# Every second step of the second layer's forgetting attention reordered to values, turning, scores; value products one step later

## What is computed

```
def fox_attention(q, k, v, Fq, Fk, q_off):          # second layer only
    def block(args):                                # one block of 128 queries
        qb, fqb, qpos = args
        s = jnp.einsum('bqhd,bkhd->bhqk', qb, k) * FOX_SCALE
        s = s + jnp.swapaxes(fqb, 1, 2)[..., None] - Fk_t
        s = jnp.where(kpos[None, :] <= qpos[:, None], s, -jnp.inf)
        p = jax.nn.softmax(s, axis=-1)
        return jnp.einsum('bhqk,bkhd->bqhd', p, v)

def mem_attend(q, k, v):                            # both layers
    p = jax.nn.softmax(jnp.einsum('blhd,bmhd->bhlm', q, k) * MEM_SCALE, axis=-1)
    return jnp.einsum('bhlm,bmhd->blhd', p, v)

x = x + jnp.concatenate([op, om], axis=-1) @ w_out[i]
x = x + swiglu(x, g_ffn[i], w_gu[i], w_down[i])
```

## Time and profile before

| | |
|---|---|
| median of 3 executions | 1226.25 us (1225.66 to 1226.43) |
| span of the profiled execution, first to last instruction | 1224.1 us |
| TensorE busy, of that span | 1208.8 us (99%) |
| VectorE, ScalarE busy | 983.7 us (80%), 649.6 us (53%) |
| second layer's attention (704.4 to 779.3 us) | 74.9 us |
| of it, one chunk of four forgetting pairs | 10.32 us |
| TensorE clock granted, mean | 0.998 of full speed |

### The profile page before, as it was taken

The page is one execution under the profiler, slowest core; times in us unless marked ns, Lnnn a source line. Parts: engine busy times, 40 slices in busy tenths (PEclk is TensorE's granted clock), DMA queues, the critical chain, the costliest instruction groups (busy, mean ns, idle before and its releaser), DMA issues.

```text
span 1224.1 us, 23230 instructions
## 1 busy us (share of the span) xinstructions
PE 1208.8 (99%) x9048; PEld 1167.6 (95%) x9048; DVE 983.7 (80%) x1605; ACT 649.6 (53%) x1175; POOL 88.9 (7%) x124
## 2 busy tenths in 40 slices
PE   8999999999999999999999999999999999999997
PEld 8998999999999999999989986899999999999997
DVE  6777558999999999976776377557999999999972
ACT  6657335454554555555754377534555555555542
POOL 2000000001001001102001100000001001100103
PEclk9999999999999999999999999999999999999999
DMA  7343222236325434525444310132134433532622
GB/s 229 121 138 106 67 74 86 74 88 141 96 87 121 109 96 106 132 86 158 138 129 124 99 40 2 36 87 86 53 101 116 114 95 96 125 104 83 163 62 86
DMA packets 198012, 124.08 MB, mean 101 GB/s; under 512 B 6419, under 2 KB 190131, under 8 KB 197648
## 3 DMA queue, kind: packets, MB, share of 16 engines
q1 hardware_dynamic: 185792, 101.23, 28.0%
q0 software_dynamic: 11920, 21.30, 7.7%
q10 hardware_dynamic: 192, 0.06, 0.0%
HBM read 106.67 MB, written 7.94 MB: 94 GB/s over the span
## 4 chain that ended last, share of the span: by engine, by line
PE 94%; DVE 2%; ACT 1%; DMA 1%; issue 1%; SPq 0%; DVEq 0%; ACTq 0%
PE ACCP L1854 32%; PE ACCP L1875 25%; PE MISC L1875 23%; PE ACCP L1967 3%; PE ACCP L2127 3%; PE ACCP L2098 2%; PE MISC L1891 1%; PE MISC L2069 1%; PE MISC L2082 1%; PE MISC L1897 1%; DMA XR<-in_x_prompt 1%; PE MISC L2086 1%; DVE XL L1579 0%; DVE ACC L1587 0%; DVE WL L1433 0%
## 5 line engine op out<-in xcount | busy, mean ns | idle before, releaser
L1102 ACT ACTIVATE WH<-RAW 128x1024 fp32r<-128x1024 f32 (+2 forms) x149 | 144.1, 967 | 140.9 <-PE ACCP L1854 120.6
L1120 ACT ACTIVATE EH<-SB 128x1024 fp32r<-128x1024 f32 (+1 forms) x116 | 112.6, 970 | 161.4 <-DVE SB L1458 80.6
L1433 DVE TENSOR_TENSOR WL<-RAW,WH 128x1024 fp32r<-128x1024 f32 (+2 forms) x148 | 166.2, 1123 | 17.5 <-ACT WH L1102 16.4
L1464 DVE TENSOR_TENSOR EL<-SB,EH 128x1024 fp32r<-128x1024 f32 (+1 forms) x116 | 128.7, 1109 | 5.5 <-ACT EH L1120 3.4
L1854 PE MATMUL ACCP<-XH,WH 128*128 128x288 f32 x512 | 111.2, 299 | 0.5 <-DVE XL L1579 0.5
L1854 PE MATMUL ACCP<-XH,WL 128*128 128x288 f32 x512 | 109.7, 296 | 0.0
L1854 PE MATMUL ACCP<-XL,WH 128*128 128x288 f32 x512 | 109.6, 296 | 0.0
L1875 PE MATMUL MISC<-BH,EH 128*128 128x288 f32 x360 | 106.7, 296 | 0.0
L1875 PE MATMUL ACCP<-BH,EH 128*128 128x288 f32 x360 | 106.6, 296 | 0.0
L1875 PE MATMUL ACCP<-BL,EH 128*128 128x288 f32 x360 | 106.2, 295 | 0.0
L1875 PE MATMUL MISC<-BL,EH 128*128 128x288 f32 x360 | 106.2, 295 | 0.0
(11 more groups left out here) (362 smaller groups left out, 3414.2 us busy)
## 6 DMA issues: line engine op xcount, KB each, us to landing
RAW<-in_w_gu SPq DMA_DIRECT2D x88, 512.0 KB, 4.1
RAW<-in_w_down SPq DMA_DIRECT2D x48, 384.0 KB, 3.9
RAW<-in_w_in SPq DMA_DIRECT2D x16, 512.0 KB, 5.1
RAW<-in_w_mem_kv SPq DMA_DIRECT2D x16, 512.0 KB, 3.7
RAW<-in_w_out SPq DMA_DIRECT2D x16, 512.0 KB, 3.9
X<-PC POOLq DMA_DIRECT2D x48, 144.0 KB, 2.9
RAW<-in_w_down SPq DMA_DIRECT2D x16, 256.0 KB, 2.7
RAW<-in_w_kv SPq DMA_DIRECT2D x8, 512.0 KB, 3.7
```

What stands on the lines that cost most here:

```text
L1102: a.activation(panel_in(WH, w % SPLIT_SLOTS, p), panel_in(RAW, p % RAW_SLOTS, p), ACT.Copy).then_inc(split_ready(w, True)[0], 1)
L1120: a.activation(EH[:, first:first + n, 0:nh], mixtures(s)[:, first:first + n, 0:nh], ACT.Copy).then_inc(block_hi, n)
L1433: v.tensor_tensor(panel_in(WL, w % SPLIT_SLOTS, p), panel_in(RAW, p % RAW_SLOTS, p), panel_in(WH, w % SPLIT_SLOTS, p), ALU.subtract).then_ ...
L1464: v.tensor_tensor(EL[:, first:first + n, 0:nh], mixtures(s)[:, first:first + n, 0:nh], EH[:, first:first + n, 0:nh], ALU.subtract).then_in ...
```

## The change

In the second layer, values and closing come one step later (values of pair n-4, closing of pair n-5), and the loop has one step more. And in each odd step whose scores are of forgetting attention (n = 11, 13, ... 29) the order is values of pair n-4, turning of pair n-2, scaling of pair n-1, and only then scores and exponentials of pair n. Even steps, memory steps and the steps behind the last scores keep scores, turning, values. The first layer is as it was.

```
-        for n in range(len(twos) + 4):
-            new, scaled, turned, valued, closed = (lag(n, by) for by in range(5))
+        late = layer == DEPTH - 1
+        for n in range(len(twos) + 4 + late):
+            new, scaled, turned = (lag(n, by) for by in range(3))
+            valued, closed = lag(n, 3 + late), lag(n, 4 + late)
+            flipped = new and new.att == "fox" and n % 2 == 1
             if closed and closed.last:
                 add("branch_hi", two=closed)
+            if flipped:
+                if valued:
+                    add("values", two=valued, g=before["g"])
+                for e in range(2):
+                    add("turn_probs", r=turned.rows[e], first=False, g=before["g"])
+                add("scale_probs", two=scaled)
             if new:
                 add("scores", two=new, m=before["jobs"], s=before["s"], g=before["g"], i=n)
                 for what in ((first, second)[n] if n < 2 else ()):
                     what()
             if closed and closed.last:
                 add("branch_lo", two=closed)
-            if scaled:
+            if scaled and not flipped:
                 add("scale_probs", two=scaled)
             for e in range(2):
                 if new:
                     add("exp", r=new.rows[e])
-                if turned:
+                if turned and not flipped:
                     add("turn_probs", r=turned.rows[e], first=turned.first and e == 0, g=before["g"])
-            if valued:
+            if valued and not flipped:
                 add("values", two=valued, g=before["g"])
```

## The result

| | before | the change |
|---|---|---|
| median of 4 executions | 1226.12 us (1225.66 to 1226.43) | 1235.34 us (1233.89 to 1235.75) |
| span of the profiled execution | 1224.1 us | 1234.0 us |
| second layer's attention, first scores to first matmul of the projection | 74.92 us | 84.74 us |
| one chunk, third to fourth (transposes of tile 3 to transposes of tile 3) | 10.32 us | 12.04 us |

The change is slower: ratio 1.0073, 95% interval 1.0061 to 1.0084, that is +9.2 us against a forecast of +7.1. The attention is 9.82 us longer and the span 9.9, so everything lies there. The projection behind it takes 56.19 us in both.

What follows compares the result with a forecast made beforehand. TensorE's own work bounds the kernel, so waits reach the end whole. 4.6 + 2.1 + 1.0 + 1.55 - 0.8 - 1.3 = +7.1 us on the 1224.1 us span: 1231.2, median 1233.3 us; range 1227.0 to 1236.5.

Steps and rivals of the forecast that it cites:

- ahead of tile 2: Transposes of tile 2 after tile 3 wait for late PT copies, 1.15 us, four times: +4.6 us.
- ahead of tile 0: Transposes of tile 0 after tile 1 wait for late PT copies, 0.69 us, three times: +2.1 us.
- at pair 13: Sample's last pair: TensorE waits for VectorE's late scaling, some 0.7 us, and 0.3 for head 1's copy: +1.0 us.
- at the last pair: Pair 29's scaling stands behind chunk 2's closing: wait 1.4 us, and 0.15 for the last values: +1.55 us.
- memory steps: Second layer's memory steps, whose copies also wait for values: costed at nothing; +1.8 us if cover failed in nine steps.
- shapes: TensorE's array-shape changes, 85 before and 82 now, priced 0.15 us, or 0.09 from whole array to rows: -1.3 us.
- old wait: Waits of before that go: 0.12 and two of 0.13 in the chunks, about 0.3 and 0.15 at the end: -0.8 us.
- The one price for every change: Whole array to rows costs 0.15 us like other shape changes: shapes give -0.5 us in place of -1.3.
- The last copy: At the attention's end, the last values wait 0.15 us, part of the end's +1.55 us.
- The copies are not late: Rival: TensorE never waits; only shape changes and old waits go, 1224.1 us, or 1222.9; faster given 0.07.
- The waits are half as long: Rival: free handovers, sample and end cost nothing: 1227.5 to 1228.8 us; no change (1223.8 to 1228.7) given 0.10.
- More is late: Rival: whole array to rows costs 0.15 (+0.8) and memory steps wait (+1.8): 1235.9 us; above 1236.5 given 0.05.

Runs made afterwards that it cites:

- Six slots: The change with six PT slots in place of four: 1229.52 us, +3.7 us against the kernel before.
- copies first: The change with both PT copies of an even forgetting step ahead of its two exponentials on ScalarE, four slots: 1230.96 us, +4.5 against before.
- undisturbed change: The change run a second time, unaltered, with the clock at 1.00 behind pair 13: 1234.73 us, +8.8 against before.
- both mended: The change with six PT slots and both copies ahead of the exponentials in even forgetting steps: 1226.16 us, -0.3 against before.
- the old order without waits: The change without its flipped steps, values and closing still one step later, with six PT slots: 1225.78 us, 0.0 against before.
- late-only version: The change without its flipped steps: values and closing one step later, four PT slots: 1231.82 us, +6.0 against before.
- grouped order: Against before: second layer's forgetting pairs in groups of two, like array shapes together, six PT slots, copies behind exponentials: 1222.92 us, -3.6.

## Why the prediction was right, and where its sizes were off

**The direction and the cause were right.** Time is TensorE's own; the change made it wait, and the waits went to the end whole. They stand where the prediction put them: ahead of tile 2 in both heads, ahead of tile 0 in the second head, at pair 13 and at the last pair; the copies of even steps are released by value products. Six slots and copies first take the chunk's waits away, one half each. One wait stands where the prediction had none: in the memory steps, 0.4 us.

**The sum by place.** Taken against the undisturbed change (+8.21 us in the attention, 83.13 less 74.92):

- *The three chunks*: forecast 1.15 + 0.69 for the waits and -0.24 for shapes (four changes of 0.15 become four of 0.09) in each, and -0.12 and -0.13 for the old wait in the second and third, 4.55 in all. Measured 5.2, of which 0.2 in the first chunk is moved work (0.65 in, 0.44 out), so 5.0. The waits, against the same order without them: from the values to the next scores 2.88 us at tile 2 against 1.61 (756.23 to 759.11; 752.07 to 753.68), so 1.27; at tile 0, 2.89 against 2.17 (749.99 to 752.88; 756.60 to 758.77), so 0.72. They were 0.15 longer than forecast together. A hand-over from ScalarE to TensorE takes 0.14 us, where I had put 0.04, a row of ScalarE to VectorE; and value products to the copy take 0.31 after the last issue (0.75 less eight products of 0.055), not 0.24.
- *Shapes and old waits*: forecast -0.36 in the second and third chunk, measured -0.26 (10.32 to 10.06). But the old order without waits also takes 10.05, so the -0.24 for the kinds of change is not there, and what went was the waits of before (0.22 and 0.06), worth twice what I took. That term failed in its split: I priced the change from the whole array to rows at 0.09 by one pair of rows behind a gate product. There it holds (0.15 less 0.06), but behind transposes it is no cheaper than the change to columns. The one price for every change that the prediction weighed, -0.5 in place of -1.3, was nearer.
- *The memory steps*: put at nothing. From the attention's first scores to the first of the sample it is 19.79 us in the change (705.20 to 724.99) and 19.40 with six slots (704.11 to 723.51). So the ring costs 0.4 us here, a little in each step and most in the last one. Its four transposes take 0.57 us to the values in the change (723.37 to 723.94) and 0.44 with six slots (722.08 to 722.52):

```profile
723.37 0.74 PE L2107 MATMUL ACCP<-IDENT,PR 128*128 128x128 f32 x4
722.08 0.60 PE L2111 MATMUL ACCP<-IDENT,PR 128*128 128x128 f32 x4
```

- *The sample and the end*: forecast 1.0 at pair 13, 1.15 + 1.55 - 0.13 - 0.45 = 2.1 at the end, and -0.6 for the changes of shape outside the chunks, 2.5 in all. Measured +0.29 (37.20 less 36.91) and +2.72 (9.77 less 7.05); with the moved work put back, +0.94 and +2.28, 3.2 in all. At pair 13 the wait is some 0.6 us, 0.39 of it idle ahead of the first head, where I had 1.0; the memory steps add 0.4. At the end the wait at tile 2 is again 1.27 and that for the last pair's scaling 1.3, where I had 1.4. The last copy costs 0.46 in place of 0.15: the last 24 value products take 1.92 us in the second run (786.41 to 788.33) and 1.46 with six slots. The old waits there were 0.66 and not 0.58. What is left for the changes of shape outside the chunks is -0.2, not -0.6.

Together 5.0 + 3.2 = 8.2 us against 7.1 forecast. The mis-sized terms are the two waits in the chunk, through the hand-overs, the gain from the shapes, of which little came, the memory steps and the last copy; pair 13, 0.4 too dear, hid a part of this.

**The clock** added 1.6 us in the profiled run of the change and nothing in the second one. It was not in the forecast. In the medians (+9.2 and +8.8) the share of each can't be told.

**The rivals.** *The copies are not late* fell: they are late by exactly the ring and the exponential. Nor was its time, 1224.1 us, what a kernel without those waits takes: with both mended it took 1226.16 us, as before. The waits at pair 13 and ahead of the last pair stay (0.39 and 1.18 us idle), and the order of shapes gives nothing in a chunk. *The waits are half as long* fell by their measured lengths. *More is late* (1235.9 us) came near the median by its number, in part by luck. Both of the reasons that it put a price on were there in part: the change to rows is no cheaper where it stands behind transposes, and the memory steps wait, but 0.4 us and not 1.8; and in the profiled run the clock added 1.6 us.

## What to carry to other kernels

A stage that is moved one step later needs buffers for one more step: count who waits for the slot to be freed before counting what the order saves; here two more slots gave back 4.8 of the 8.2 us that the attention had lost. On an engine that works in order, what stands between two copies belongs to the wait of the second one's reader. And when the engine that bounds the kernel pays 0.11 us for each change of array shape, put like with like across pairs (12 changes a chunk became 6; with the old waits, which went too, -3.6 us), after making sure that nothing waits.

## What the runs showed of the hardware that was not expected

- From the end of a ScalarE copy to the TensorE transposes that wait for it: 0.14 us (757.58 to 757.72, 758.52 to 758.66, and the same in the late-only version).
- A fall of the granted clock from 1.00 to 0.50 (2.4 to 1.2 GHz) for some 3.5 us, behind an idle stretch of 0.39 us, cost 1.6 us. With the same idle stretch (0.39 and 0.40 us) at the same place it came neither in the second run nor with six slots nor with copies first. An execution of the late-only version, which has no such stretch there, took 1234.62 us at a mean granted clock of 0.995, the other three 1231.53 to 1231.86 at 0.998 and 0.999; it has no trace. What decides it stays open.
- The price of a change of array shape: 0.11 us each by the grouped order (0.68 us in a chunk for six), below the 0.15 read from single rows. The Trainium skill, TensorEngine Tiling (Array Packing), Key Properties, says that a change of tiling mode drains TensorE; the runs agree that fewer changes are faster.
- The waits view names the releaser that ended last: for the second head of tile 2 that was a scaling which the transposes don't need. The start 0.14 us behind the copy, and its going when the copy was moved, decided it.
